# Up projections of 18 block pairs a layer as seven quarter products: weight sums by accumulating DMAs, activation sums by VectorE, and an FFN in four chunk groups

## The reference, cut to what matters

```python
def conv_ffn(h, buf, w_up, w_dw, b_dw, w_down):
    g, val = jnp.split(h @ w_up, 2, axis=-1)
    g, tail = causal_depthwise_conv(g, buf, w_dw, b_dw)
    return (jax.nn.gelu(g) * val) @ w_down, tail
```

## Time and profile before

| | us |
|---|---|
| median of 3 runs | 1453.04 (1452.38 to 1454.13) |
| the profiled execution | 1455.54 |
| its span | 1453.9 |
| TensorE busy | 1421.9 (98%), clock granted 0.999 |
| VectorE, ScalarE, GpSimd busy | 982.1, 905.8, 275.3 |
| read from HBM | 262.80 MB |

### The profile page before, as it was taken

One profiled execution on the slowest core, in us unless ns is written; L12 is line 12 of the kernel. 1 busy time (PEld: TensorE's weight loads), 2 busy tenths in 40 slices (PEclk: granted clock), 3 DMA queues, 4 the chain that ended last, 5 costly groups with the idle time before them and its releaser, 6 DMA issues.

```text
span 1453.9 us, 28797 instructions
## 1 busy us (share of the span) xinstructions
PE 1421.9 (98%) x11346; PEld 1317.7 (91%) x11346; DVE 982.1 (68%) x1443; ACT 905.8 (62%) x1743; POOL 275.3 (19%) x440
## 2 busy tenths in 40 slices
PE   5999999999999999999999999999999999999998
PEld 4777758999999999999989977679999999999997
DVE  5889975887754688744635558865878744877643
ACT  4699977767644677643624558865776643766543
POOL 2488920000000232200000033210000000322200
PEclk9999999999999999999999999999999999999999
DMA  9877684254554445554425458863345554454652
GB/s 379 324 286 293 238 293 136 78 184 160 167 192 160 144 164 163 177 189 147 159 73 199 179 203 283 298 235 119 115 162 172 183 180 133 160 173 161 198 167 99
DMA packets 72119, 273.53 MB, mean 188 GB/s; under 512 B 8064, under 2 KB 10128, under 8 KB 71600
## 3 DMA queue, kind: packets, MB, share of 16 engines
q1 hardware_dynamic: 65824, 247.69, 50.0%
q0 software_dynamic: 5872, 23.64, 4.8%
q10 hardware_dynamic: 288, 0.35, 0.1%
HBM read 262.80 MB, written 8.85 MB: 187 GB/s over the span
## 4 chain that ended last, share of the span: by engine, by line
PE 83%; DVE 7%; DMA 3%; ACT 2%; issue 2%; SPq 1%; POOL 1%; POOLq 0%; DVEq 0%; ACTq 0%
PE ps L749 70%; DVE ps L1941 4%; PE ps L1020 3%; DMA ada_w<-w_ada_dram 2%; DMA ada_y<-w_ada_dram 1%; PE ps L1079 1%; PE ps L1116 1%; PE ps L1138 1%; PE ps L1177 1%; PE ps L1154 1%; PE ps L724 1%; PE ps L819 1%; DVE y L1961 1%; PE ps L935 1%; PE ps L1029 1%
## 5 line engine op out<-in xcount | busy, mean ns | idle before, releaser
L1772 DVE TENSOR_TENSOR w_lo<-raw,w_hi 128x1024 fp32r<-128x1024 f32 (+1 forms) x296 | 387.9, 1311 | 228.7 <-ACT w_hi L1291 228.1
L749 PE MATMUL ps<-h_hi,w_hi 128*128 128x288 f32 x1920 | 525.2, 297 | 1.7 <-DVE h_lo L1846 1.7
L749 PE MATMUL ps<-h_lo,w_hi 128*128 128x288 f32 x1920 | 519.3, 295 | 0.0
L1291 ACT ACTIVATE w_hi<-raw 128x1024 fp32r<-128x1024 f32 (+1 forms) x309 | 347.1, 1124 | 102.4 <-PE ps L749 72.0
L749 PEld LDWEIGHTS ps<-h_hi,w_hi 128*128 128x128 f32 x1920 | 360.2, 188 | 8.2 <-DVE h_lo L1846 4.5
L749 PEld LDWEIGHTS ps<-h_lo,w_hi 128*128 128x128 f32 x1920 | 360.0, 188 | 1.1 <-issue 0.2
L749 PE MATMUL ps<-h_hi,w_lo 128*128 128x288 f32 x1920 | 312.8, 294 | 0.1
L749 PEld LDWEIGHTS ps<-h_hi,w_lo 128*128 128x128 f32 x1920 | 274.4, 188 | 0.4 <-DVE w_lo L1772 0.4
L749 PE MATMUL ps<-act_pair,w_hi 128*128 128x288 f32 x1408 | 207.0, 295 | 0.0
L749 PEld LDWEIGHTS ps<-act_pair,w_hi 128*128 128x128 f32 x1408 | 194.4, 188 | 0.0
L2123 DVE SCALAR_TENSOR_TENSOR cv<-g_pad,par,cv 128x224 f32<-128x224 f32 (+1 forms) x176 | 85.3, 485 | 45.8 <-ACT cv L1548 40.9
(11 more groups left out here) (241 smaller groups left out, 1920.5 us busy)
## 6 DMA issues: line engine op xcount, KB each, us to landing
raw<-w_k_dram SPq DMA_DIRECT2D x245, 512.0 KB, 3.5
raw<-w_down_dram SPq DMA_DIRECT2D x64, 704.0 KB, 4.1
ada_w<-w_ada_dram SPq DMA_DIRECT2D x71, 512.0 KB, 6.0
k_page<-cache_kt_dram SPq DMA_DIRECT2D x32, 512.0 KB, 5.4
v_page<-cache_v_dram POOLq DMA_DIRECT2D x32, 512.0 KB, 5.2
ada_h<-w_ada_dram SPq DMA_DIRECT2D x7, 512.0 KB, 7.1
ada_u<-w_ada_dram SPq DMA_DIRECT2D x6, 512.0 KB, 15.1
ada_g<-w_ada_dram SPq DMA_DIRECT2D x6, 512.0 KB, 5.9
```

Of the source, the lines that this page charges most:

```text
L749: return pe.matmul(ps[:, BANK[b], 0:HALF], lhsT=w[s][:, kb * P:(kb + 1) * P], rhs=v[:, at, :] if down else v[:, at, lo:hi], start=(at == 0 ...
L1291: act.activation(w_hi[SLOT[n]][:, 0:cols], raw[s][:, 0:cols], ACT.Copy).then_inc(s_hi, 1)
L1772: dve.tensor_tensor(w_lo[s][:, 0:cols], raw[n % RING][:, 0:cols], w_hi[s][:, 0:cols].bitcast(F32), ALU.subtract).then_inc(s_lo, 1)
```

## The change: what it does

Per layer the first 4 pairs (`PLAIN`) of gate and value chunk are computed as before, now 8 up blocks of half 0, then 8 of half 1. The other 18 pairs are computed once for all 576 tokens by a seven-product scheme on quarters. The output of a pair is a 2x2 matrix of blocks (gate or value; token half 0 or 1), the inner dimension is cut in two halves of four kb; W(n, k) is the quarter 128 x 512 of chunk n (0 gate, 1 value) and inner half k, h(k, t) the quarter of the activations. Products 1, 2, 3 and 4 use W or one weight sum, and products 5, 6, 7 sums on both sides:

- weight sums: buffer `w_chain` is loaded with W(1,0); an accumulating DMA of POOL adds W(1,1) (product 5), after its low part is made another adds W(0,0) (product 6), and another W(0,1) (product 3). `w_column` is W(0,0) with W(1,0) added (product 7). Products 1, 2 and 4 use plain quarters, in halves of `raw`. Weights are only added; the signs lie in the activation sums and in two copies with scale -1. Each quarter is loaded with its own DMA of 256 KB: 9 a pair, 4 of them accumulating.
- activation sums: VectorE makes four of them (`t_sums`) after value blocks of half 1, from y, where norm steps 2 and 5 now leave the unrounded h; ScalarE and VectorE split them (`t_round`, `t_low`) during the first down part. The fourth overwrites h(0, 1).
- on TensorE a product is 4 kb x 3 matmuls (`product`). The seven of a pair interleave with the pair before in the order of `CYCLE`. Pairs alternate between banks 0 to 3 and 4 to 7. ScalarE and VectorE copy and add the products between PSUM and SBUF (`keep_one`, `keep_five`, `keep_two`, `add_five_seven`, `drain_first`, `drain_last`), then the convolution, gelu and product run on 576 columns (`last_tap`, `second_tap`, `third_tap`, `pair_gate`, `pair_product`, `pair_hi_row`, `pair_low_row`). Roundings and low parts of weight quarters run six products ahead of TensorE.
- the down projection is cut in four groups of 4, 5, 5 and 8 chunks (`PART_CHUNKS`), each after its pairs. In the first three the 16 blocks alternate the token halves, so that each weight is loaded once; ScalarE copies each result to y, and before a block of the next group back into the PSUM bank (`bring_back`), where the matmuls go on adding. At a group's begin four blocks (three in the last group) run without their last chunk first.
- the chains of half 1 in front of the FFNs and of half 0 behind FFN 0 are tight now; `x_stat` of half 1 is put inside the 8th up block. `spread_steps` is gone. The ring's buffers are 128x1024.

In the diff below the first `pair_group` is ScalarE's program, the second VectorE's, and `add_quarter` is POOL's.

```diff
+PLAIN = 4
+PART_CHUNKS = (PLAIN, 5, 5, 8)
+COMBOS = 2 * RING
+T_ORDER = (5, 7, 6, 4)
+CYCLE = ((5, 0), (1, 0), (7, 1), (2, 0), (3, 1), (6, 0), (4, 1))
...
     def ffn(layer, row):
         for h in range(2):
-            for i in range(FC):
+            for i in range(PLAIN):
                 for s in range(2):
                     out.append(Block("up", layer, 2 * i + s, h, 0, C, row + 2 * i + s, 2 * i + s))
-            for n in range(C):
-                for part in range(2):
-                    out.append(Block("down", layer, n, h, part, FH, (2 * layer + part) * C + n, n))
+        for g, k in enumerate(PART_CHUNKS):
+            if g < PARTS - 1:
+                order = [(n, h, n) for n in range(C) for h in range(2)]
+            else:
+                order = [(n, 0, n) for n in up] + [(n, 1, pos) for pos, n in enumerate(down)]
...
+        if half:
+            return Chain(r, half, norm, ended, 0, (3, 3, 4, 4), (4, 4, 5, 5), (5, 5, 6, 6), 7, 7, True)
         return Chain(r, half, norm, ended, 1, (2, 2, 3, 3), (3, 3, 4, 4), (4, 4, 5, 5), 6, 6, True)
-    return Chain(r, half, norm, ended, 2, (4, 7, 10, 13), (5, 8, 11, 14), (9, 12, 15, 16), 18, 20, False)
...
+            def product(gid, q):
...
+                if role == 5:
...
+                    if a == 0 and j < 2:
+                        for _, k, count in GROUP_HELD[gid]:
+                            pe.wait_ge(bank_free[k], count)
+                    if j >= 2:
+                        pe.wait_ge(last_gate, m - 1)
+                elif role == 1:
+                    if j >= 2:
+                        pe.wait_ge(two_copied, m - 1)
+                elif role in (6, 2):
+                    pe.wait_ge(one_copied, m + 1)
+                elif role == 7:
+                    pe.wait_ge(two_copied, m + 1)
+                elif role == 3:
+                    pe.wait_ge(five_copied, m + 1)
+                else:
+                    pe.wait_ge(both_added, m + 1)
+                if role in T_ORDER:
+                    pe.wait_ge(t_lo, T_LO_FROM + 4 * layer + T_ORDER.index(role) + 1)
+                pe.wait_ge(combo_lo, 7 * PAIR_FROM[gid] + q + 1)
...
+            def pair_group(gid):
...
+                for c in range(last):
+                    if c >= 1:
+                        set_edge(m0 + c - 1)
+                    of(pair_gate, c - 2)
+                    of(keep_one, c)
+                    rounds(c, 0, 1)
+                    of(pair_hi_row, c - 2)
+                    of(keep_five, c)
+                    of(last_tap, c - 1)
+                    of(keep_two, c)
+                    rounds(c, 2, 3, 4, 5)
+                    if c >= 1:
+                        keep_tail(m0 + c - 1)
+                    rounds(c, 6)
+                    of(drain_first, c)
...
+            def pair_group(gid):
...
+                for c in range(last):
+                    lows(c, 0, 1)
+                    of(add_five_seven, c - 1)
+                    of(pair_low_row, c - 2)
+                    of(drain_last, c - 1)
+                    of(second_tap, c - 1)
+                    lows(c, 2, 3)
+                    of(third_tap, c - 1)
+                    lows(c, 4, 5, 6)
+                    of(pair_product, c - 1)
...
+            def add_quarter(n):
+                role, m = ADD_ORDER[n]
+                if n >= ADDS:
+                    pool.wait_ge(add_done[n % ADDS], ADD_FROM[n % ADDS] + 16 * (n // ADDS))
+                if role == 5:
+                    pool.wait_ge(chain_in[m % 4], CHAIN_FROM[m % 4] + 16 * (m // 4 + 1))
+                    out, src = w_chain[m % 4], quarter_of_w(m, 1, 1)
+                elif role == 6:
+                    pool.wait_ge(combo_lo, PRODUCT_AT[5, m] + 1)
+                    out, src = w_chain[m % 4], quarter_of_w(m, 0, 0)
+                elif role == 3:
+                    pool.wait_ge(combo_lo, PRODUCT_AT[6, m] + 1)
+                    out, src = w_chain[m % 4], quarter_of_w(m, 0, 1)
+                else:
+                    pool.wait_ge(column_in[m % 2], 16 + 16 * (m // 2 + 1))
+                    out, src = w_column[m % 2], quarter_of_w(m, 1, 0)
+                pool.dma_start(out[:], src, accum_op=ALU.add).then_inc(add_done[n % ADDS], 16)
```

More of the change, by code:

```diff
@@ L734, in one_half @@
                 whole = ready is None and kbs is None
+                back = down and bl.part > 0
                 kbs = range(bl.k) if kbs is None else kbs
@@ L959, in next_block @@
                     ready = lambda kb: norm_wait(5 if bl.layer else 2, kb, bl.half)
-                elif bl.phase == "down" and bl.pos == 0:
-                    ready = lambda kb: pe.wait_ge(act_ready, (2 * bl.layer + bl.half) * FC + bl.part * FH + kb + 1)
-                before = [c for c, ch in enumerate(CHAINS) if ch.norm in (2, 5) and not ch.half and b - ch.ended == ch.x_stat + 1]
+                before = [c for c in STAT_INSIDE if b - CHAINS[c].ended == CHAINS[c].x_stat + 1]
                 if before:
@@ L2171, in after_block @@
                 split_ahead(b)
+                for gid, q in AHEAD.get(b, ()):
+                    combo_low(gid, q)
                 if bl.phase == "up" and bl.unit % 2:
                     gated_lo(b)
+                if bl.phase == "up" and bl.half and bl.unit % 2:
+                    t_sums(bl.layer, bl.unit // 2)
+                if bl.phase == "down" and bl.part == 0 and bl.pos < T_ROWS and not bl.half:
+                    t_low(bl.layer, bl.pos)
                 if b == 2 * C + 2:
```

726 lines of the change are left out of this document (600 added, 126 removed).

## The result

The changed kernel takes **1478.47 us** (median of 4 runs, 1477.2 to 1479.67) against 1452.84 (4 runs of the kernel before on the same chip): ratio 1.0175 [1.0157, 1.0192], 25.6 us slower. The profiled execution has a span of 1475.3 us, 21.4 more than before.

A forecast was written before the change was run, and what follows sets the result against it. TensorE's matmuls were taken to bound the kernel. From 1455.5 us, less 57.2 saved, plus 3 leaks, 24 late norm, 8 lag and 10.5 groups gave 1443.8; 2.5 lower for the median, 1441 us, range 1420 to 1468.

The forecast's parts named there:

- What the change takes away: Pairs of both layers: 432 matmuls fewer at 0.1325 us each, 57.2 us saved, all on the path.
- The steady pair: Middle of the groups: TensorE's 11.1 us a pair covers ScalarE, VectorE and a 10.0 us engine loop; 3 us leaks.
- The plain chunks: Plain up blocks and first down part: VectorE's late norm costs 24 us, the lag at the down part 8 us.
- The weight sums: POOL's accumulating quarter loads: landing in 5 us plus 0.6 for the issue, hidden while the two stay under 7 us.
- The six groups: Begins and ends of the pair groups: bare copies, raw-buffer reload, bank reloads and a drain, together 10.5 us (0 to 25).
- the additions decide: Rival, chance 0.12: quarter 6's addition sets the pair's period once issue plus landing pass 6.9 us; slower, 1479 at 8 us.
- The loop of the engines is longer: Rival, chance 0.19: the 10.0 us loop through three engines is 1.5 to 2.1 longer in steady pairs; 1454 to 1473.

The follow-up runs named there:

- e4: Changed kernel with the 12 matmuls of product 5 done twice in each pair, 432 more in all: 1529.2 us, ratio 1.0523.
- e1: Changed kernel with idle matmuls put where TensorE waited in the up stage, in both layers: 1483.79 us, ratio 1.0205.
- e2: Changed kernel with VectorE's work before the late norm cut short (fewer columns, numbers wrong), about 11.5 us a layer: 1467.71 us, ratio 1.0080.
- e3: Changed kernel with POOL's 144 accumulating DMAs made plain copies of the same sizes (weight sums wrong): 1465.76 us, ratio 1.0076.
- e7: Changed kernel with product 4's weight quarter exchanged with product 1's in the raw ring, in layer 0's second group alone: 1473.03 us, ratio 1.0149.
- e9: Changed kernel with six plain pairs, two groups of 8, and half 1's chain before each FFN spread over more up blocks: 1473.07 us, ratio 1.0130.
- e17: Changed kernel with seven plain pairs, groups of 7 and 8, chain spread, half 1's norm cut up behind three blocks: 1466.91 us; with norm in one go 1456.89.
- e6: Changed kernel with five weight low parts a layer, after up blocks 2 to 6, made by GpSimd instead of VectorE: 1490.97 us, ratio 1.0272.
- e8: e9 with nine low parts of weights a layer made by GpSimd: 1496.1 us, ratio 1.0293.
- after: The changed kernel itself, as its runs and trace show it, against the kernel before: 1478.47 us, ratio 1.0175.

## Why the prediction was wrong, step by step

- **What the change takes away**: right. 432 matmuls fewer; e4 prices them at 0.117 us in the reverse direction, and the mechanism, matmuls on the path, holds in every group's middle.
- **The steady pair**: right. 84 matmuls, no wait, all three engines fit under TensorE. The 3 us for leaks in the steady cycles were hardly needed: the last group of eight loses 1.0 us, half of it in its first cycle.
- **The plain chunks**: the mechanism was right and nearly the size: VectorE was to have the first h_lo at 307.4 and had it at 308.9, with the waits at block 7, the statistics and h_lo where I had put them, 9.6 and 9.1 us (I had 12 a layer), and 3.0 and 2.8 at the first down part (I had 4). The stages cost 37.6 instead of 32. What I had no term for is the clock after a wait; e1 shows that it adds little as long as VectorE is late anyway. That VectorE's queue alone makes it late was too simple: e2 took 11.5 us out of it and over half of the waits stayed, since statistics to first h_lo is a chain of some 7 us by itself.
- **The weight sums**: mis-sized. I took 5 us to landing and called it hidden, with 7 as the limit in the steady state. The additions land after 6.2 and 7.2 us (medians). The steady state bears that; the first cycles of a group, where all three engines start at once and nothing runs ahead, do not. I had priced those cycles only for one bare copy each (3 us; it measured 0.5 in each of the six groups, as I had it). e3: 12.7 us in the medians, 8.9 in the pairs of the table; e4 takes 7.8 off the same cells.
- **The six groups**: the step of the sum that failed most. 10.5 + 3 us stood against 31.7 (39.7 in the table less 8 for the next point). 4.5 of it was to be the reload of the raw buffer behind the last product 4. That mechanism was right too, as e7 shows; but I had one first and two second places where there are one and three, and a second place costs 2 us, not 1: 9.3 us. Of the 39.7 us 26.5 are waits: these 9.3, the bare copies 2.9, late additions in the second cycles 5.6 (above), the first weights of the next group 2.2 (at 554.88), x_sum of the next point 3.3, small ones the rest. Clock is at most 5.1 (half of three stretches of 3.4 us); what is left goes to matmuls a little over 0.1325 us and to starts after a wait.
- **Not in the sum at all**: the chain of half 0 behind FFN 0 is tight now and stands beside half as many down blocks. TensorE waits 3.3 us for x_sum, with 3.4 us at half clock behind it: the last down part loses 9.6 us in layer 0, 1.6 in layer 1, where no such chain follows. 8 us that the diff's own line on the chains announced, though 1.6 of them are waits at the group's own end, and a wait of 2.0 for y_sum with another 3.4 us at half clock lies behind the stage, among the keys. This is read from the trace; no run took the chain away.

5.6 for the plain stages, 18.2 for the groups (31.7 where 10.5 + 3 stood) and 8 for that chain make 31.8 of the 33.1 us I was short. Of the rivals, *the additions decide* named the right part, but at a place where it doesn't decide: its limit, 11.1 less 4.3, is 6.8 us (not 6.9), and the steady pairs show no wait for a sum. *The loop of the engines is longer* is refuted: the steady pair takes 84 x 0.1332 = 11.2 us without a wait. The result lies in a sum of small edges that no rival held, and outside my range.

Open: why groups of eight have no late `keep_one` in the second cycle where groups of five and seven have; why e1 and e2 lost in groups that they didn't touch; and how much of the groups' loss is clock alone, since no run took it away there without taking the waits. It is at most the 5.1 us above.

## What to carry to other kernels

Here a scheme that saves work in the steady state was paid for at its edges: count the edges (here six group begins, six ends, two norms that lost their cover, one chain more), price each from the order of in-order queues with nothing running ahead, and only then the middle. Fewer, longer groups were worth more than the matmuls they gave back. And here the late engine was not relieved by cutting its work up (e9, e17) or by giving it to GpSimd (e6, e8): both were tried, and both were slower.

## What the runs showed of the hardware

- A GpSimd subtraction of 128x1024 takes 2.4 to 2.95 us (VectorE: 1.22), and VectorE instructions with two SBUF inputs beside it end 0.3 to 0.6 us after it: 0.75 us becomes 2.97 (e6).
- An accumulating DMA of 256 KB lands 2.5 us later than the same copy (6.2 against 3.7, medians of 108 in after and e3).
- In after the granted clock is at 0.5 in seven stretches, 44 us together, each in or behind waits of TensorE; before the change, with next to no wait in the FFNs, once, for 3.4 us. With idle matmuls in the waits (e1) it stayed at 1.00 where after had 0.64, and the stage took as long.
